# A decoder block on one core: the second token tile's attention and projections are set between the first tile's expert rows

## The reference

```python
qry = (h @ w_q).reshape(B, T, PEER_HEADS, 2, half)
s = jnp.einsum('bthpd,hpnd->bthpn', qry, sub_keys)
s1, i1 = lax.top_k(s[:, :, :, 0], PEER_TOPK)
s2, i2 = lax.top_k(s[:, :, :, 1], PEER_TOPK)
...
act = jax.nn.gelu(jnp.einsum('cd,ced->ce', hs, u[es]))
return jnp.einsum('ce,ced->cd', gs * act, v[es])
```

## Time and profile before

| | us |
|---|---|
| median of 3 runs | 2354.93 (2353.43 to 2355.19) |
| the profiled execution | 2352.66 |
| its span in the profile | 2350.9 |

### The profile page before, as it was taken

How to read it: one execution, slowest core, us unless ns; L and a number is a source line. 1 busy time by engine, 2 the same in 40 slices (tenths; PEclk the granted TensorE clock), 3 DMA queues, 4 the chain that set the end, 5 groups by cost and what they waited for, 6 DMA issues and landing times.

```text
span 2350.9 us, 17146 instructions
## 1 busy us (share of the span) xinstructions
PE 1936.5 (82%) x5571; PEld 997.9 (42%) x5571; DVE 1302.4 (55%) x2208; ACT 439.4 (19%) x995; POOL 727.5 (31%) x656
## 2 busy tenths in 40 slices
PE   1789999999999999997878677867777786778776
PEld 0334564444456777873333233323333332333232
DVE  6756224665165657567555655475375556555642
ACT  0001011222234444332101100110221112111100
POOL 2112000000000000016554454445364545554450
PEclk8789889999999999998989888888878898889888
DMA  9978636776575564379999999999999999999995
GB/s 342 367 270 325 211 105 201 266 247 236 157 245 177 195 238 160 125 269 398 422 421 422 422 422 422 422 422 422 422 396 422 422 422 422 422 422 422 422 422 240
DMA packets 161483, 774.93 MB, mean 330 GB/s; under 512 B 15028, under 2 KB 21352, under 8 KB 86036
## 3 DMA queue, kind: packets, MB, share of 16 engines
q0 software_dynamic: 91648, 637.57, 66.9%
q1 hardware_dynamic: 67684, 132.80, 16.7%
q10 hardware_dynamic: 2096, 3.85, 0.4%
HBM read 772.04 MB, written 2.13 MB: 329 GB/s over the span
## 4 chain that ended last, share of the span: by engine, by line
PE 53%; DMA 34%; DVE 7%; issue 3%; POOL 1%; ACT 1%; DVEq 0%; ACTq 0%; POOLq 0%; SPq 0%
DMA arena<-in_peer_v_dram,idx_now 28%; PE PS L1268 22%; PE PS L878 14%; DMA arena<-in_ada_w_dram 3%; PE PS L871 2%; PE PS L873 2%; PE PS L872 2%; PE PS L1255 2%; DVE arena L1332 2%; DVE arena L1386 1%; PE PS L1051 1%; DMA w_raw<-in_peer_w_q_dram 1%; POOL arena L529 1%; DMA arena<-in_cmp_w_dram 1%; PE PS L1037 1%
## 5 line engine op out<-in xcount | busy, mean ns | idle before, releaser
L1268 PE MATMUL PS<-arena 128*128 128x512 f32 x2048 | 983.1, 643 | 282.9 <-DMA arena<-in_peer_v_dram,idx_now 261.5
L1777 DVE CUSTOM_DVE_ANT_0 arena<-arena 128x2048 f32<-128x2048 f32 x256 | 582.6, 2291 | 448.3 <-DMA arena<-in_peer_u_dram,idx_now 447.8
L1268 PEld LDWEIGHTS PS<-arena 128*128 128x128 f32 x2048 | 419.9, 208 | 845.5 <-issue 807.2
L529 POOL DMA_INDIRECT arena<-in_peer_v_dram,idx_now x256 | 360.1, 1407 | 425.0 <-PE PS L1268 340.6
L878 PE MATMUL PS<-arena 128*128 128x512 f32 (+1 forms) x912 | 407.3, 592 | 0.0
L529 POOL DMA_INDIRECT arena<-in_peer_u_dram,idx_now x256 | 289.9, 1132 | 215.4 <-DVE dots L1777 119.4
L878 PEld LDWEIGHTS PS<-arena 128*128 128x128 f32 x912 | 168.2, 192 | 174.9 <-issue 168.3
L461 POOL DMA_DIRECT2D arena<-in_ada_w_dram x64 | 34.0, 532 | 487.1 <-DVE arena L1386 274.2
L824 ACT ACTIVATE act_g<-dots 128x4 f32<-128x4 f32 x64 | 13.2, 206 | 912.6 <-DVE dots L1777 912.6
L1589 DVE TENSOR_TENSOR w_lo<-w_raw,w_hi 128x1024 fp32r<-128x1024 f32 x96 | 116.2, 1224 | 110.8 <-ACT w_hi L714 110.2
L1386 DVE SCALAR_TENSOR_TENSOR arena<-arena,csil 128x2048 f32<-128x2048 f32 x60 | 141.1, 2351 | 13.9 <-DMA arena<-in_ada_w_dram 12.0
(11 more groups left out here) (259 smaller groups left out, 1649.9 us busy)
## 6 DMA issues: line engine op xcount, KB each, us to landing
arena<-in_ada_w_dram POOLq DMA_DIRECT2D x96, 1024.0 KB, 5.8
arena<-in_w_in_dram SPq DMA_DIRECT2D x112, 512.0 KB, 5.7
w_raw<-in_w_out_dram SPq DMA_DIRECT2D x32, 512.0 KB, 4.1
w_raw<-in_peer_w_q_dram SPq DMA_DIRECT2D x32, 512.0 KB, 3.7
w_raw<-in_w_branch_nsa_dram SPq DMA_DIRECT2D x16, 512.0 KB, 4.3
w_raw<-in_w_branch_mla_dram SPq DMA_DIRECT2D x16, 512.0 KB, 3.6
arena<-in_x_dram SPq DMA_DIRECT2D x4, 1024.0 KB, 6.3
arena<-in_cmp_w_dram SPq DMA_DIRECT2D x8, 512.0 KB, 11.0
```

The lines of the kernel that those rows point to most:

```text
L529: pool.indirect_dma_start(ring[e % RING], None, tab, bass.IndirectOffsetOnAxis(ap=idx_now[:, now, e:e + 1], axis=0)).then_inc(landed[e % R ...
L1268: ins = nc.tensor.matmul(PS[:, bank + k, :], diag[e % 8], Vrow[e % RING][:, k * NC:(k + 1) * NC], start=(first and e == 0), stop=False, sk ...
L1777: v.tensor_tensor_reduce(row, row, h2[:, t, :], 1.0, 0.0, ALU.mult, ALU.add, dots[:, e:e + 1]).then_inc(u_free, 1)
```

## The change

- Attention units are now two heads of one tile (`score(t, n)`, `turn(t, n)` and so on), 16 + 8 units a tile. Before the experts only tile 0's units run; each has both weight tiles' gate products (eight matmuls) and two ada rows. V of both branches is kept aside (`v_keep`, four POOL copies), since `proj` is overwritten.
- The three projections use f32 matmuls of the weights as loaded (`mix`), for one tile: two matmuls of 128x512 a weight tile. The split in high and low parts is gone. For tile 0 the weights use the ring of eight; for tile 1 all 96 weight tiles are loaded again, in a ring of four (`w2ring`), and four rows more.
- Norm, queries and scores are done for tile 0, then its 128 U and 128 V rows run in 132 slots written out one by one, with five buffers each (`RING0`). PE takes V row s-4 in slot s. Slots 0 to 55 hold tile 1's attention, a unit in two slots (mostly), slots 56 to 92 its branch and output projections (7 weight tiles in 4 slots), 93 to 101 norm and transposes, 102 to 117 the query projection (2 tiles a slot), then last scores. On each engine the steps of a slot stand in one fixed order.
- Tile 1's expert rows run as before with eight buffers; tile 0's final norm (`finish(0)`) stands in their first unit.

```diff
 RING = 8
+RING0 = 5
 BATCH = 4
 
 WSLOTS = 8
+W2SLOTS = 4
 ADA_SLOTS = 4
...
+        LAG = 4
+        SLOTS = PH * TOPK + LAG
+        MIX1 = 2 * UNITS + 8
+
+        def unit_slot(n):
+            return 2 * n if n <= NSA_UNITS else 2 * n + 4
+
+        def head_slot(p, hh):
+            return unit_slot(NSA_UNITS + p) - 2 + hh if p else hh
+
+        NORM = MIX1 + 63 * 4 // 7 + 1
+        H2_SLOT = NORM + 7
+
+        def mix_slot(i):
+            return MIX1 + i * 4 // 7 if i < 64 else H2_SLOT + 2 + (i - 64) // 2
+        TOPK_AT, GEXP_AT = (1, 4, 7, 10), 8
...
+            for i in range(MIX):
+                load(W_BR + i, mix_src(i))
+                if i == 7:
                     sp.wait_ge(ada_cols, 2 * QTRS + 4)
                     sp.wait_ge(mod_stored, 16)
-                    sp.dma_start(gate_a_row, mod_dram[0, :].partition_broadcast(P)).then_inc(row_in, 16)
...
+            sp.wait_ge(weighed, 2 * UNITS)
+            for i in range(MIX):
+                if i >= W2SLOTS:
+                    sp.wait_ge(w2_used, i - W2SLOTS + 1)
+                sp.dma_start(w2ring[:, i % W2SLOTS, :, :], mix_src(i)).then_inc(w_landed[i % W2SLOTS], 16)
+                if i == 7:
+                    mod_row(gate_a_row[1], 0, row_in[1])
+                if i == 39:
+                    sp.wait_ge(merged_ready, 8)
+                    sp.dma_start(X[1], x_v[:, 1, :]).then_inc(x2_in[1], 16)
+                    mod_row(scale_f_row[1], 2, scale_in[1])
+                if i == 67:
+                    sp.wait_ge(y_mul, 8)
+                    mod_row(shift_f_row[1], 1, shift_in[1])
+            sp.wait_ge(h2_ready[1], 1)
+            mod_row(gate_f_row, 3, last_row_in)
             for t in range(NT):
...
+            pool.wait_ge(pj_out, 3)
+            pool.wait_ge(cmpx_ready, 2)
+            for t in range(NT):
+                for b in range(2):
+                    v0 = KV0 + ((b + 1) * 2 + 1) * GROUPS * HD
+                    pool.tensor_copy(v_keep[:, t, b, :], proj[:, t, v0:v0 + GROUPS * HD]).then_inc(vkeep_ready, 1)
...
+            def u_row0(i):
+                u, e = i // TOPK, i % TOPK
+                if e == 0:
+                    take(u, u % 2)
+                if i >= RING0:
+                    pool.wait_ge(u0_free, i - RING0 + 1)
+                elif i == 0:
+                    pool.wait_ge(merged_ready, 4)
+                elif i == 1:
+                    pool.wait_ge(y_mul, 4)
+                elif i == 4:
+                    pool.wait_ge(x1_ready[0], 1)
+                else:
+                    pool.wait_ge(h2_ready[0], 1)
+                fetch(u_tab, Urow0[i % RING0], u % 2, e, u_in[i % RING0])
+
+            def v_row0(i):
+                if i >= RING0:
+                    pool.wait_ge(v0_free, i - RING0 + 1)
+                else:
+                    pool.wait_ge(w_used, W_BR + MIX - 6 + 2 * min(i, 3))
+                fetch(v_tab, Vrow0[i % RING0], i // TOPK % 2, i % TOPK, v_in[i % RING0])
+
+            for i in range(PH * TOPK):
+                if i >= RING0:
+                    v_row0(i - RING0)
+                u_row0(i)
...
+            def second_attention(s):
+                for n in range(UNITS):
+                    if s == unit_slot(n) + 2:
+                        softmax_exp(1, n)
+                    if s == unit_slot(n) + 5 and (n >= NSA_UNITS or n % 4 == 3):
+                        out_out(1, n // 4 if n < NSA_UNITS else GROUPS + n - NSA_UNITS)
+                for p in range(PAIRS):
+                    for hh in range(2):
+                        if s == head_slot(p, hh):
+                            heads_out(1, p, hh)
+                for n in range(UNITS):
+                    if s == unit_slot(n) + 3:
+                        probs_out(1, n)
+
...
+                    if u == 0:
+                        act.wait_ge(sc_out, 4)
+                    if u + 1 == PH:
+                        act.wait_ge(sc_out, 5)
+                    fetch(scores[(u + 1) // PH][:, (u + 1) % PH, :])
+                if s % BATCH == 0 and b:
+                    act.wait_ge(coef_ready, b)
+                    if b > 2:
+                        act.wait_ge(v0_free, (b - 2) * BATCH)
+                    diags(range((b - 1) % 4 * BATCH, (b - 1) % 4 * BATCH + BATCH))
...
-                            ins = split_product(PS[:, 4 * (c_ % 2) + 2 * t + w // 4, :], oT_hi[:, j, cols], oT_lo[:, j, cols],
-                                                w_hi[:, m % SPLIT, k, :], w_lo[:, m % SPLIT, k, :],
-                                                start=(kk == 0), stop=(kk == 7))
-                    ins.then_inc(w_used, 1)
...
+            def score(t, n):
+                u, K = t * UNITS + n, (t + 1) * P
...
+                if t == 0:
+                    tile_ready(W_BR + i)
+                    tile, used = wring[:, (W_BR + i) % WSLOTS, :, :], w_used
+                else:
+                    pe.wait_ge(w_landed[i % W2SLOTS], w2_landed(i))
+                    tile, used = w2ring[:, i % W2SLOTS, :, :], w2_used
+                for k in range(2):
+                    ins = nc.tensor.matmul(PS[:, 4 + j % 3, :], lhs[:, 2 * w + k, :], tile[:, k, :],
+                                           start=first and k == 0, stop=last and k == 1)
+                ins.then_inc(used, 1)
...
+            def v_row0(i):
+                pe.wait_ge(v_in[i % RING0], 16 * (i // RING0 + 1))
+                pe.wait_ge(diag_ready, i + 1)
+                for k in range(4):
+                    ins = nc.tensor.matmul(PS[:, k, :], diag[i % 8], Vrow0[i % RING0][:, k * NC:(k + 1) * NC],
+                                           start=(i == 0), stop=False, skip_group_check=True)
+                ins.then_inc(v0_free, 1)
...
+            def second_attention(s):
+                for n in range(UNITS):
+                    if s == unit_slot(n) + 4:
+                        weigh(1, n)
+                    if s == unit_slot(n) + 3:
+                        turn(1, n)
+                for n in range(UNITS):
+                    if s == unit_slot(n):
+                        score(1, n)
+                for p in range(PAIRS):
+                    for hh in range(2):
+                        if s == head_slot(p, hh):
+                            pe.wait_ge(mt_out, PAIRS + 2 * p + hh)
+                            turn_head(1, p, hh).then_inc(mt_in, 1)
+
+            pe.wait_ge(q_nat, 4)
+            pe.wait_ge(sc_out, 4)
+            for s in range(SLOTS):
+                if s < MIX1:
+                    second_attention(s)
+                if s == MIX1:
+                    pe.wait_ge(o_out, 2 * OUTS)
+                for i in range(MIX):
+                    if mix_slot(i) == s:
+                        mix(1, i)
+                if s == H2_SLOT:
+                    pe.wait_ge(h2_ready[1], 1)
+                    for g in range(4):
+                        turn_h2(g)
+                if s == QTR_SLOT:
+                    turn_queries(1, 3)
+                if s == SC_SLOT:
+                    score_experts(1, 3)
+                if s >= LAG:
+                    v_row0(s - LAG)
...
+            for n in range(NSA_UNITS):
+                if n % 8 == 0:
+                    mod_out(n // 8)
+                mask_max(0, n)
+                ada_row(KD + 2 * n)
+                normalise(0, n)
+                ada_row(KD + 2 * n + 1)
...
+            def dot0(i):
+                dve.wait_ge(u_in[i % RING0], 16 * (i // RING0 + 1))
+                row = Urow0[i % RING0]
+                v.tensor_tensor_reduce(row, row, h2[0], 1.0, 0.0, ALU.mult, ALU.add,
+                                       dots[:, i % TOPK:i % TOPK + 1]).then_inc(u0_free, 1)
+
+            for s in range(SLOTS):
+                u, e = s // TOPK, s % TOPK
+                if u < PH:
+                    if e == 0:
+                        if u:
+                            dve.wait_ge(coef_ready, u * 4)
+                        link(v.tensor_copy(gate_now[:, :], gate_next[:, :]))
+                        parts = topk_parts(u + 1)
+                    dot0(s)
+                if s < MIX1:
+                    second_attention(s)
+                second_projections(s)
+                if u < PH:
+                    if e in TOPK_AT:
+                        parts[TOPK_AT.index(e)]()
+                    if e % BATCH == BATCH - 1:
+                        coefs(u, e // BATCH)
```

More of the change, by code:

```diff
@@ L815, in unit @@
[L815 to L831 removed]
+            act.wait_ge(gate_out, 7)
@@ L1856, in _ @@
+            unit(0, first=True)
+            with dve.Fori(0, PH - 2) as r:
+                ch.enter(r, TOPK_STEPS + 1)
+                unit(r + 1)
+                ch.leave(PH - 2)
+            unit(PH - 1, last=True)
             finish(1)
```

1341 lines of the change are left out of this document (668 added, 673 removed).

## The result

The changed kernel takes 2341.0 us (median; 2332.9 to 2347.1) against 2355.2 for the kernel before, measured beside it: ratio 0.9929, 95% interval 0.9916 to 0.9942. It is faster by 0.7%, some 17 us by the ratio and 14 by the two medians; the forecast was 25 us, to 2330. The profiled execution took 2335.3 us with a span of 2333.6, so it lies low among its runs; the forecast span was 2326.

The account below looks back on a forecast made before the run. Expert rows were taken as transfer-bound, 386 to 1064 us as PE-bound. Gathers' start 831 + gathers 1274 + store and gap 6 + tail 44 + tile 1's bytes 141 + slots 30 = 2326 us span, 2330 measured; range 2262 to 2398.

Parts of the forecast that it names:

- Projections of tile 0, 93 and its bound of 108: Tile 0's branch and output projections: weight transfer sets the time, 76 + 14 + 3 = 93 us, bounds 80 and 108.
- 4.8 us: Tile 0's first attention: PE time a unit, 3.4 for eight matmuls at 0.43 plus 1.4 for small ones.
- under 4.5 us: Attention slots: PE time a slot for four V matmuls and half a unit, against 4.97 us of DMA.
- Query projection, 33 us: Tile 0's query stage: 24 weight tiles at 1.36 us, first eight loaded under the norm; 8 us more pass.
- Late next in that stage is a weight tile: Tile 0's query projection: a weight tile named as the next thing to be late; no size given.
- Latent attention, 80: Tile 0's MLA stage: 8 units of 9.2 us and a tail of 6, 80 us where it was 103.
- Attention slots, 10 us charged: Slots with tile 1's attention beside tile 0's gathers: 10 us lost beyond the bytes, bounds 0 and 80.
- The count of DVE, 19.4 of 19.9 us: Attention slots: DVE needs 19.4 us per four slots against 19.9 of DMA, so DMA still binds, barely.
- Slots with weights, 20 us charged, and 131 for the bytes: Tile 1's projections: reloading 96 tiles at 1.36 us costs 131; PE waits and serial norm 20, bounds 5 and 70.
- the slow one: Rival: the slots go at DVE's pace, 24 us per four attention slots for 19.9; 2409 us measured, chance 0.24.
- Starving: Rival: slots with weights get a fifth of the DMA, 6.2 us a tile; 2511 us measured, chance 0.04.
- The faster rival: Rival: bytes alone set attention units at 7.7 us, slots lose 10 us for 30; 2274 us measured, chance 0.2.

Follow-up runs that it names:

- The later gather: Changed kernel, but the first U gather starts only when TensorE has used all but the last eight weight tiles of the first load: 2321.2 us, ratio 0.9861.
- The wide tiles: Changed kernel, but 64 of tile 1's 96 weight tiles cut as one row of 1024 columns, 4 KB packets for 2 KB, same bytes: 2323.0 us, ratio 0.9853.

## Why the prediction was right, and where not

The sign and the mechanism held: engine time comes out of 386 to 1064 us, bytes go into a full DMA, and the difference is small. The forecast span of 2326 missed the 2333.6 by 8 us, as the sum of larger errors. Projections and query stage were 33 us too short, latent attention and norm 14 too long, and what tile 1 pays 11 too long; that they nearly cancel is luck:

| term | forecast | measured |
|---|---|---|
| start of stage behind tile 0's first attention | 531 | 531.0 |
| compression stage | 72 | 72 |
| latent attention | 80 | 70 |
| projections of tile 0 | 93 | 115.7 |
| norm | 14 | 10 |
| query projection and wait | 33 + 8 | 51 |
| start of the gathers | 831 | 850 |
| bytes and slots of tile 1 | 141 + 30 | 160 |

The measured start of the gathers, and with it the 51, is worked out as in the prediction: 892 us, less 12.7 MB of rows gathered before it (30 us at 421.5 GB/s; the gather queue from 836 to 892 us, packets, MB, share, stands below), less the 12 to 13 us by which transfers outlast the mark from which the 44 us of tail are counted, here as in the kernel before. The 160 are what then remains of 2333.6 - 850 - 1274 - 6 - 44.

```profile
q0 software_dynamic: 1744, 12.72, 56.6%
```

*Projections of tile 0, 93 and its bound of 108: the step that failed.* The prediction gave PE 128 x 0.43 = 55 us and so took the transfers for the bound. The 0.43 was read from x64 in 27.52 us as if an entry were a matmul. The stage needs 110 us of PE for its products alone and took 115.7; the transfers, with half of the matmuls away, gave 98. The same error stands in "4.8 us" an attention unit of tile 0 (8.5 to 9.4 by the chain), in "under 4.5 us" an attention slot (PE is busy for 257.68 of the 268 us from 892 to 1160) and in "3.5 us" a weight slot. In the slots the full DMA hid it; in tile 0's units it did so for the first half only. So PE too was near its limit in the attention slots, which the prediction said of DVE alone. One look at a line of known count would have caught it: four matmuls a row times 256 rows are 1024, not 2048.

*Query projection, 33 us.* The same error (32 tiles are 55 us of PE), and one more: the prediction had nothing queued beside its weights, though in the changed kernel the first five U gathers are issued from 836 to 842 us, before the last of these weights at 843. The later gather prices that, with the hole behind it, at 16 us. "Late next in that stage is a weight tile" was right, for a reason I did not give.

*Latent attention, 80.* The stage was forecast 10 us too long: at a DMA share of 0.87 the ada rows in its chain landed in 6.0 to 8.8 us. Which part of the 8 x 9.2 + 6 was too dear was not tried. This gain, and the norm's, pay for 14 of the projections' 23 us.

*Attention slots, 10 us charged.* 413 for 421.5 GB/s over 268 us are 5.4. The count of DVE, 19.4 of 19.9 us, was too high: it was busy for 0.73 of the time. Part of the excess is 2.3 us a four slots of waits on ACT that I had counted as DVE's own time.

*Slots with weights, 20 us charged, and 131 for the bytes.* 53.6 MB at 421.5 are 127 us, and 398 for 421.5 GB/s over 500 us are 28 more: 155 beside 161 charged. I had the cost of the 2 KB packets as a transfer of its own (1.36 us a tile) and order on top. The wide tiles bring back 11 of the 24 GB/s, with two thirds of the weights in 4 KB packets, so about half of the loss is shown to be the packets; whether the rest is the third still in 2 KB packets, the 4 KB of the others or the order of the slots, no run tells.

Rivals: the slow one did not happen; with 68.7 us more on DVE its path opens, at 16 us of its 79. Starving did not either; PE waited for weights for 14 and 16 us at a time while rows used the time. The faster rival's 7.7 us a unit was out of reach, since PE needs 8.5 to 9.4.

Of the signs named beforehand, the 53.6 MB and the full DMA in the slots came as stated. The rates were 413 and 398 GB/s for 421 and 410, and a weight tile each 1.36 us until 800 and V matmuls near 835 did not come: PE set the first, the late weight and the hole the second.

## What to carry to other kernels

Before a duration from a profile is multiplied, its count of entries is set against a count that the code gives; one entry is not always one instruction. Once the DMA is full to the end of a kernel, a change is priced by the bytes moved before that point and the rate behind it. Work on the engines behind it was free here up to what was tried (with PE busy for 0.98 of a stretch the DMA stayed full; DVE at 0.92 cost 16 us), and the shape of a weight tile was not. Prefetching into short rings before their consumer can run takes the queue from the loads that the consumer waits for.

## What was unexpected of the hardware

- A 128x512 f32 matmul took 0.86 us and is recorded as two entries of 0.43; three passes on split halves took about 0.71 a product in the kernel before.
- Beside 8 KB gathers, weights in 2 KB packets pulled the whole DMA from 422 to 398 GB/s; with two thirds of them in 4 KB packets it was 409, at a share of 1.00 and 1.01. The share doesn't show this loss, only the GB/s do.
- A ring of four rows did as well as five. The time from issue to landing followed the depth: 22.4 us with eight buffers, 11.4 and 9.4 with five.
- 512 KB of weights, 3.7 us from issue to landing at the median in the query projection of the kernel before, took up to 24 us behind five gathers of 1.05 MB.
